# A router that reads rows without their reciprocal root, in a two-layer fp32 decoder trunk with a mixture of experts

## The reference, cut to what matters

```python
def rmsnorm(x, g):
    xf = x.astype(jnp.float32)
    y = xf * lax.rsqrt(jnp.mean(xf * xf, axis=-1, keepdims=True) + EPS)
    return (y * g.astype(jnp.float32)).astype(x.dtype)

def moe_swiglu(h, router, w_gate, w_up, w_down):
    logits = jnp.einsum('bsd,de->bse', h, router).astype(jnp.float32)
    vals, idx = lax.top_k(logits, TOP_K)
    gates = jax.nn.softmax(vals, axis=-1)
    combine = jnp.sum(jax.nn.one_hot(idx, N_EXPERTS, dtype=jnp.float32) * gates[..., None], axis=-2)
    y = jnp.zeros_like(h)
    for e in range(N_EXPERTS):
        y = y + combine[..., e:e + 1].astype(h.dtype) * swiglu(h, w_gate[e], w_up[e], w_down[e])
    return y
```

## Time and profile before

| | |
|---|---|
| median of 3 runs | 1526.59 us (1522.37 to 1526.75) |
| profiled execution | 1525.41 us, of which the span of instructions is 1523.5 us |
| TensorE busy in the span | 1490.9 us (98%) |
| VectorE, ScalarE busy | 1156.9 us (76%), 965.7 us (63%) |
| mean granted TensorE clock | 0.994 |
| router stretch, from the last wide product of the mixer to the first expert unit | 499.39 to 516.37 us |

### The profile page before, as it was taken

How to read it: one execution, slowest core, us unless ns; L and a number is a source line. 1 busy time by engine, 2 the same in 40 slices (tenths; PEclk the granted TensorE clock), 3 DMA queues, 4 the chain that set the end, 5 groups by cost and what they waited for, 6 DMA issues and landing times.

```text
span 1523.5 us, 20125 instructions
## 1 busy us (share of the span) xinstructions
PE 1490.9 (98%) x7134; PEld 1235.0 (81%) x7134; DVE 1156.9 (76%) x948; ACT 965.7 (63%) x854; POOL 11.0 (1%) x21
## 2 busy tenths in 40 slices
PE   8999999999899999999999999999999999999997
PEld 6788888887778888888888888888888888888885
DVE  4565544454547688898888888888889888888886
ACT  4554444343444677777777767777777777776775
POOL 0100000000000000000000000000000000000000
PEclk9999999999999999999999999999999999999999
DMA  9623555555450499999989989999999998999992
GB/s 354 243 96 118 200 189 176 190 189 173 158 166 16 159 342 377 329 345 366 373 317 370 371 311 359 388 330 352 372 335 347 375 364 320 362 374 324 365 378 111
DMA packets 184089, 433.61 MB, mean 285 GB/s; under 512 B 6963, under 2 KB 8011, under 8 KB 184060
## 3 DMA queue, kind: packets, MB, share of 16 engines
q1 hardware_dynamic: 182048, 426.80, 78.2%
q0 software_dynamic: 1776, 5.84, 1.2%
q10 hardware_dynamic: 236, 0.57, 0.1%
HBM read 432.10 MB, written 1.09 MB: 284 GB/s over the span
## 4 chain that ended last, share of the span: by engine, by line
PE 91%; DVE 4%; ACT 2%; issue 1%; DMA 1%; DVEq 0%; ACTq 0%; POOLq 0%
PE ps L1158 27%; PE ps L1160 27%; PE ps L1159 27%; PE ps L1325 2%; DVE wlo L696 2%; PE ps L1473 2%; ACT whi L425 1%; PE ps L1279 1%; PE ps L1252 1%; PE ps L1165 1%; PE ps L1265 1%; PE ps L1177 1%; DMA gain<-in_mem_norm 1%; PE ps L1497 0%; PE ps L1225 0%
## 5 line engine op out<-in xcount | busy, mean ns | idle before, releaser
L696 DVE TENSOR_TENSOR wlo<-raw,whi 128x2048 fp32r<-128x2048 f32 x404 | 918.6, 2289 | 241.9 <-ACT whi L425 241.7
L425 ACT ACTIVATE whi<-raw 128x2048 fp32r<-128x2048 f32 x404 | 772.1, 1914 | 248.1 <-PE ps L1160 247.1
L1158 PE MATMUL ps<-whi,xhi 128*128 128x512 f32 x1328 | 520.4, 392 | 6.5 <-DVE wlo L696 5.5
L1159 PE MATMUL ps<-wlo,xhi 128*128 128x512 f32 x1328 | 517.0, 389 | 0.0
L1160 PE MATMUL ps<-whi,xlo 128*128 128x512 f32 x1328 | 516.8, 389 | 0.0
L1158 PEld LDWEIGHTS ps<-whi,xhi 128*128 128x128 f32 x1328 | 249.8, 188 | 63.4 <-DVE wlo L696 11.0
L1160 PEld LDWEIGHTS ps<-whi,xlo 128*128 128x128 f32 x1328 | 250.0, 188 | 51.9
L1159 PEld LDWEIGHTS ps<-wlo,xhi 128*128 128x128 f32 x1328 | 250.1, 188 | 50.5
L1158 PE MATMUL ps<-whi,thi 128*128 128x512 f32 x560 | 224.2, 400 | 2.9 <-DVE tlo L877 2.9
L1160 PE MATMUL ps<-whi,tlo 128*128 128x512 f32 x560 | 218.8, 391 | 0.0
L1159 PE MATMUL ps<-wlo,thi 128*128 128x512 f32 x560 | 218.3, 390 | 0.0
(11 more groups left out here) (171 smaller groups left out, 701.9 us busy)
## 6 DMA issues: line engine op xcount, KB each, us to landing
raw<-in_moe_up SPq DMA_DIRECT2D x112, 1024.0 KB, 6.7
raw<-in_moe_gate SPq DMA_DIRECT2D x112, 1024.0 KB, 6.1
raw<-in_moe_down SPq DMA_DIRECT2D x112, 1024.0 KB, 6.2
raw<-in_ffn_up SPq DMA_DIRECT2D x14, 1024.0 KB, 5.1
raw<-in_ffn_gate SPq DMA_DIRECT2D x14, 1024.0 KB, 5.2
raw<-in_ffn_down SPq DMA_DIRECT2D x14, 1024.0 KB, 4.9
raw<-in_dil_w_in SPq DMA_DIRECT2D x10, 1024.0 KB, 5.0
raw<-in_swa_w_in SPq DMA_DIRECT2D x4, 1024.0 KB, 15.7
```

The costliest lines, as they stand in the source:

```text
L425: act.activation(whi[:, c % CUT, 0:span(c)], raw[:, c % RAW, 0:span(c)], ACT.Copy).then_inc(hi_ready, 1)
L696: dve.tensor_tensor(wlo[:, c % CUT, 0:n], raw[:, c % RAW, 0:n], whi[:, c % CUT, 0:n].bitcast(F32), ALU.subtract).then_inc(lo_ready, 1)
L1158: pe.matmul(dst, ahi, bhi, start=start, stop=False)
L1159: pe.matmul(dst, ahi, blo, start=False, stop=False)
```

## The change

The row's number rstd is no longer multiplied into hn. hn is now h * gain, written by `gained` (line 716 before) without waiting for the root; ScalarE multiplies rstd in when it writes `nhi`, VectorE when it writes `nlo`. The logits come out without it; their order within a token is the same, since it is positive, and it goes into the differences from which the gates are made. ScalarE's squares go to `silu` as scratch, not to hn. TensorE turns both tiles before the first logit, with two `keep_warm` products in place of the seven that stood up to the last logit.

```diff
-                elif k < 4:
+                elif k < 5:
                     scratch = silu[:, :, :].rearrange("p t f -> p (t f)")
...
+            def n_hi(t):
+
                 act.wait_ge(hn_done, 9 + t)
-                act.activation(nhi[:, t, :], hn[:, t, :], ACT.Copy).then_inc(nhi_ready, 1)
+                act.wait_ge(rstd_done, 9 + t)
+                act.activation(nhi[:, t, :], hn[:, t, :], ACT.Copy, scale=rstd[:, 8 + t:9 + t]).then_inc(nhi_ready, 1)
+
+            route_root(0)
+            n_hi(0)
+            route_turned(0)
+            route_root(1)
+            route_turned(1)
+            n_hi(1)
             preload(ACT.Exp)
...
-            act.wait_ge(top_in, 1)
+            act.wait_ge(top_in, 2)
...
-            norm(4, 0, h)
+            gained(4, 0, h, ev_dve, DVE_EV[-1] - 2)
+            root(4, 0)
             chunk_add(C_DO, 1)
             chunk_add(C_DO + 1, 1)
-            norm(4, 1, h)
+            gained(4, 1, h, ev_dve, DVE_EV[-1])
...
-                dve.tensor_tensor(nlo[:, t, :], hn[:, t, :], nhi[:, t, :].bitcast(F32), ALU.subtract)\
-                    .then_inc(nlo_ready, 1)
+                dve.scalar_tensor_tensor(nlo[:, t, :], hn[:, t, :], rstd[:, 8 + t:9 + t], nhi[:, t, :].bitcast(F32),
+                                         ALU.mult, ALU.subtract).then_inc(nlo_ready, 1)
...
             n_lo(0)
+            root(4, 1)
...
-            dve.tensor_tensor(ex, l3, free(top, (1, 2), (0, NE)), ALU.subtract).then_inc(top_in, 1)
+            dve.wait_ge(rstd_done, 10)
+            for t in range(TILES):
+                dve.tensor_scalar(ex[:, t, :], l3[:, t, :], top[:, t:t + 1], rstd[:, 8 + t:9 + t], ALU.subtract, ALU.mult)\
+                    .then_inc(top_in, 1)
             n_lo(1)
...
             pe.wait_ge(rw_in, 16)
-            for t in range(TILES):
-                if t > 0:
-                    keep_warm(B_LG[1], 5)
-                norm_transposed(4, T_ROUTE, t)
-                keep_warm(B_LG[1], 1)
+            norm_transposed(4, T_ROUTE, 0)
+            keep_warm(B_LG[1], 2)
+            norm_transposed(4, T_ROUTE, 1)
+            for t in range(TILES):
                 for kt in range(KT):
```

More of the change, by code:

```diff
@@ L595, in _, with route_root, route_turned @@
             preload(ACT.Sqrt)
-            for t in range(TILES):
+            def route_root(t):
                 act.wait_ge(ev_dve, DVE_EV[-1] - 2 + 2 * t)
                 norm_root(4, t, h)
+            def route_turned(t):
                 for b, half in token_banks(T_ROUTE, t):
```

## The result

| | before | changed |
|---|---|---|
| median | 1524.69 us (22 runs) | 1529.41 us (22 runs) |
| lowest to highest | 1522.00 to 1528.02 | 1521.57 to 1534.42 |
| ratio of the runs | | 1.0028, 95% interval 1.0015 to 1.0042 |
| profiled execution | 1525.41 us, span 1523.5 | 1521.75 us, span 1519.9 |
| first transposes to first expert unit in it | 499.39 to 516.37, 16.98 us | 496.41 to 512.77, 16.36 us |

The changed kernel is slower by 4.7 us in the median (0.31%; the ratio of the runs says 0.28%), while its profiled execution is 3.7 us faster than that of before. Both are true. Its 22 times fall into two groups with nothing in between: eleven from 1521.6 to 1527.6, a band like that of before, and eleven from 1531.2 to 1534.4. The profiled execution is of the first group. The median of 22 lies between the groups, so it tells little; the share of the second group is the result.

A forecast was written before the change was run, and what follows sets the result against it. TensorE was taken to bound the kernel, so only the expert part's start could move: -2.09 + 0.18 = -1.9 us with the clock held, but +0.3 us with a likely short clock fall, 1526.9 us, range 1522.8 to 1531.8.

The forecast's parts named there:

- The start of the expert part reaches the end: Expert part: TensorE bounds it, so a microsecond won or lost before the first unit reaches the end unchanged.
- Tile 1's hn without the root, 3.45 us earlier: Router, before tile 1's transposes: hn no longer waits for the root, tile 1 turned at 501.55 instead of 505.00.
- Logits 2.09 us earlier: Router, both tiles turned first: -3.45 us and +1.36 us, so logits end at 506.20 instead of 508.29.
- Behind the logits, +0.18 us: Ranking and tile 1's split on VectorE: two small operations for one, plus a longer split, between 0.1 and 0.3 us.
- the sum with the clock held: Whole kernel, clock as it was: -2.09 + 0.18 = -1.9 us.
- The clock falls, between 504.5 and 507.5: Router logits: with fewer wide products beside narrow ones, TensorE's granted clock falls in most executions.
- What a fall costs: Router, from the logits on: narrow products take nearly double at 0.50; a short fall was put between -0.4 and +1.5 us.
- the short fall: Likeliest case, chance 0.43: clock falls around the logits, cold stretch of 3.4 us, +0.3 us taken, 1526.9 us.
- the long fall: Rival, chance 0.22: clock stays down through ranking and gather until the experts' wide products, +2.9 to +8.4 us, 1529.5 to 1535.0.
- the 4.6 that I called slower: Whole kernel: within 0.3%, 4.6 us, counts as no change; slower was given 0.13, same 0.84, faster 0.03.
- the range of 1522.8 to 1531.8: Total time over the cases: from the holding clock less 1.9 us for spread up to the middle of the long fall.
- The clock holds, the rival with 0.27: Router, chance 0.27: the granted clock stays at 1.00 throughout, -1.9 us, 1524.7 us.

The follow-up runs named there:

- e11: The changed kernel run again with nothing altered, one of three repeats with a trace, compared with the kernel before: 1532.60 us.
- e12: The changed kernel run again with nothing altered, another of the three repeats with a trace, compared with the kernel before: 1527.42 us.
- the root alone: Kernel before with the root out of hn, TensorE's order and its five keep_warm products between the tiles kept: 1525.01 us against 1525.10, ratio 0.9999.
- the order alone: Kernel before with both tiles turned ahead of the logits and two keep_warm products, hn still waiting for the root: 1538.57 us against 1524.87, ratio 1.0065.

## Why the prediction was right, and where its sizes were off

**The start of the expert part reaches the end.** Right: in all four traced executions of the changed kernel the total follows the router stretch and the falls ahead of it, to 0.1 us (1008.9 to 1009.0 us behind the first unit, as before; 1.9 more in e11, where the first 3.8 us are at half speed); in the slow one TensorE is busy 969.96 of 972 us behind it.

**Tile 1's hn without the root, 3.45 us earlier.** Right: 2.20 us behind tile 0's turn where I had 2.16.

**Logits 2.09 us earlier.** Right where the clock falls only behind them: 8.94 - 6.81 = 2.13 us. In e11 and e12 it fell within them, and they ended 7.15 and 7.33 us behind the first transposes against 6.63 (starts of the `keep_warm` behind them).

**Behind the logits, +0.18 us.** Too small, and the row of the changed kernel shows where (VectorE: the last ranking operation, the two small ones, the split):

```profile
505.00 0.17 DVE L1028 TENSOR_SCALAR rt<-rt 128x16 f32<-128x16 f32 x1
505.08 0.48 DVE L1031 TENSOR_SCALAR rt<-rt,stats 128x8 f32<-128x8 f32 x2
505.47 1.28 DVE L1004 SCALAR_TENSOR_TENSOR nlo<-hn,stats,nhi 128x1024 fp32r<-128x1024 f32 x1
```

The two small operations hold the split back by 0.39 us, against 0.09 for the one of before (510.20 to 510.29 in the earlier trace rows), and the split is 0.06 longer: +0.36. It counts where the clock holds: with three products between the tiles TensorE then waits for it ahead of the last wide products before the gather,

```profile
508.89 1.13 PE L1184 MATMUL ps<-mats 128*128 128x256 f32 x4 [0.29 <-DVE nlo L1004]
```

which it did not before. So the sum with the clock held was -1.9 and is -1.7, as the version with one product between the tiles shows (15.28 against 16.98), though in another order.

**The clock falls, between 504.5 and 507.5.** Right in all four executions seen: I had it 5.1 to 8.1 us behind the first transposes, and it came 7.5, 6.7, 6.0 and 5.9 us behind them. That the missing wide products do it, and not the root or its waits, is shown from both sides: with four more of them and the same wait of 0.30 us the traced execution holds its clock and none of 12 is slow, the root alone makes none slow, and taking five of them out of the old kernel brings a fall. How narrow a product must be, and whether the transposes count as narrow, is not shown.

**What a fall costs.** The price of the short fall was right: I had -0.4 us for a fall at the end of the logits, and 16.36 - 16.98 is -0.6; I had +1.5 for 6.8 us, and e12 has +1.0. The price of the long fall was right too: I had +2.9 to +8.4, and in e11 the distance is 22.73 - 16.98 = +5.75 us, with half of the 3.8 us from the first unit to 525.5 on top: +7.6. The term that failed is the chance of it: I gave the short fall 0.43 and the long one 0.22, because wide products ended the second fall of the earlier trace rows after 3.4 us. By their times and mean clocks, half the executions had the long one. Behind the logits stand only 2.2 us of wide products, then ranking and gather, which are narrow again. In e11 those products took 4.4 us at half speed and did not end the fall; it ended 3.8 us into the experts' wide products, as it did in the order alone (528.66 to 532.5). With eight of them in place of five none of 12 executions is slow. This is why the change, that was to be near zero or a loss, is a loss: +4.7 us in the median, just over the 4.6 that I called slower, and 0.28% by the ratio, just under the 0.3%.

Two sizes in the working of the long fall do not add up: its lower end leaves out 0.3 us of `keep_warm` behind the gather, the terms of its upper end give about +8.0 and not +8.4, and the middle of 1529.5 and 1535.0 is 1532.2 and not 1531.8. Nothing hangs on them.

**The number 1529.4.** It lies in the range of 1522.8 to 1531.8 by luck. It is the middle of 1527.59 and 1531.24, where no execution lies: one more execution in either group would have moved the median by 1.8 us. Only eight of the 22 times lie in the range; ten lie above it and four below. I also started from a median of 1526.59 of three runs, where 22 runs have 1524.69: the change forecast was +0.3 us, and the measured one is +4.7.

**The clock holds, the rival with 0.27.** Wrong: it fell in all four executions seen, though TensorE had been busy for 7.19 of 7.49 us. The Trainium skill, in "Perfetto Trace Analysis", section "Matmul Optimizations", says that TensorE scales its power by how much it is used, so that products should run back to back in batches. The measurement decides against reading it so for narrow products: the order that batches both tiles' logits let the clock fall, and the one that breaks them up with wide products was slow in 0 of 12 runs against 11 of 22.

What stays open: why one execution of the changed kernel has the short fall and the next the long one. The moment of the fall differs by a microsecond or two against the program (from 1.4 us before the end of the logits to 0.9 behind), but no run controls it. Nor did any run try the logits with the router as the wide operand.

## What to carry to other kernels

- `keep_warm` products that fill a wait cost nothing and may hold the clock for the whole chain behind them. When a change removes the wait, count what wide work is left beside the narrow work, not whether TensorE is busy.
- Spread what is left: one wide product between each two narrow groups, three in all, held the clock where two ahead of all the logits did not, at nearly the same length. Which of the two, the number or the place, did it was not tried.
- For a change of a few us in 1500, look at all the times and not at the median and one profile: the profiled execution was the second fastest of 22 and said "faster", while eleven of the others were 9.5 to 12.7 us slower.

## What the runs showed of the hardware that was not expected

- Once at 1.2 GHz, TensorE can stay there without any idle time: 27.3 us at 0.50 with TensorE busy 27.30 of them, in the order without the earlier hn. Its work there was transposes, 32 logit records, 4.4 us of `keep_warm`, ranking, gather and the first 3.8 us of the experts' wide products.
- The times of the kernel before spread over 7 us (1521.1 to 1528.5 over all its runs). Profiled executions differ in the falls of the clock in code that is the same in all: at 110 us 10.2, 6.8 or 0 us long, near 390 us 3.4 or 6.8, in one also at 55.8 us, in one at 482 us. That these make the whole spread was not tried.
- Two VectorE operations on 128x8, with two per-row operands each, took 0.48 us together and held the next one back by 0.39; one on 128x16 with a broadcast operand held it back by 0.09.
